# Sample attention: one gather per sequence for the cached pages, its first data fetched during the prompt's attention

## The reference

```python
def page_step(carry, pg):
    phys = page_table[:, pg]
    cos, sin = rope_tables(pg * PAGE_SIZE + jnp.arange(PAGE_SIZE))
    k, v = mla_keys(pool_ckv[layer, phys], pool_kpe[layer, phys], cos, sin, w_ukv, g_kn)
    s = jnp.einsum('bqhd,bkhd->bhqk', q, k) * SCALE
    return update(carry, s, v), None
```

## Time and profile before

| what | value |
|---|---|
| median of 3 runs | 4077.51 us (4075.68 to 4077.66) |
| the profiled execution's own time | 4077.87 us |
| its span in the trace | 4076.2 us |
| TensorE busy, share of the span | 3731.2 us, 92% |
| prompt attention | 1679 to 2212.9 us of the span |
| sample attention, setup | 2212.9 to 2261.6 us |
| sample attention, sequences and tail | 2261.6 to 2755.2 us |

### The profile page before, as it was taken

One profiled execution on the slowest core, in us unless ns is written; L12 is line 12 of the kernel. 1 busy time (PEld: TensorE's weight loads), 2 busy tenths in 40 slices (PEclk: granted clock), 3 DMA queues, 4 the chain that ended last, 5 costly groups with the idle time before them and its releaser, 6 DMA issues. The chain is left out here.

```text
span 4076.2 us, 76494 instructions
## 1 busy us (share of the span) xinstructions
PE 3731.2 (92%) x30291; PEld 2436.7 (60%) x30291; DVE 2036.8 (50%) x3709; ACT 1347.8 (33%) x2324; POOL 545.1 (13%) x809
## 2 busy tenths in 40 slices
PE   7879999999999999699997798886999998799899
PEld 4546666666666666466665455554777777455444
DVE  5773234444333333366564466654666665233353
ACT  4431013232232332255453455543545544000000
POOL 1000000000000000011112555512111121000000
PEclk9989999999999999899998899987999999899999
DMA  4422112222222221311212111104111111523342
GB/s 151 109 67 59 63 64 79 75 77 79 73 79 75 77 79 57 90 43 43 53 31 53 42 47 41 45 23 144 37 43 43 43 27 23 179 101 119 117 143 91
DMA packets 313767, 293.64 MB, mean 72 GB/s; under 512 B 90647, under 2 KB 274605, under 8 KB 300109
## 3 DMA queue, kind: packets, MB, share of 16 engines
q1 hardware_dynamic: 296572, 263.16, 20.9%
q0 software_dynamic: 14544, 25.46, 2.2%
q10 hardware_dynamic: 2304, 0.26, 0.0%
HBM read 181.38 MB, written 107.42 MB: 71 GB/s over the span
## 5 line engine op out<-in xcount | busy, mean ns | idle before, releaser
L325 PE MATMUL z_acc<-z_hx,ahead_ws 128*128 128x352 f32 x1872 | 558.0, 459 | 0.0
L543 DVE TENSOR_TENSOR z_st<-z_st,z_acc 128x1056 f32<-128x1056 f32 x208 | 254.0, 1253 | 589.0 <-PE z_acc L325 589.0
L325 PEld LDWEIGHTS z_acc<-z_hx,ahead_ws 128*128 128x128 f32 x1872 | 355.7, 190 | 198.1
L325 PE MATMUL z_acc<-hT,ahead_ws 128*128 128x352 f32 x1248 | 376.9, 459 | 0.0
L325 PE MATMUL z_acc<-hT,ahead_wt 128*128 128x352 f32 x1248 | 373.4, 459 | 0.0
L1166 PE MATMUL a_S<-a_kh,a_qb 96*128 96x512 f32 (+3 forms) x640 | 283.8, 538 | 38.2 <-DMA a_kh<-kT 29.4
L325 PEld LDWEIGHTS z_acc<-hT,ahead_ws 128*128 128x128 f32 x1248 | 236.8, 190 | 135.5 <-issue 7.7
L325 PEld LDWEIGHTS z_acc<-hT,ahead_wt 128*128 128x128 f32 x1248 | 237.1, 190 | 132.1
L1493 PE MATMUL s_kn<-s_wuk,s_ckT 128*128 128x512 f32 x528 | 293.4, 638 | 6.4 <-ACT s_sq L1571 5.0
L415 ACT ACTIVATE z_st<-z_acc 128x1056 f32<-128x1056 f32 x104 | 103.7, 1050 | 448.9 <-PE z_acc L325 448.9
L2689 PE MATMUL m_acc<-branches_o,m_wb 128*128 128x424 f32 (+1 forms) x640 | 231.2, 523 | 21.2 <-DMA m_wb<-in_w_ob 21.2
(11 more groups left out here) (401 smaller groups left out, 6470.8 us busy)
## 6 DMA issues: line engine op xcount, KB each, us to landing
ahead_wt<-in_w_in SPq DMA_DIRECT2D x52, 512.0 KB, 5.1
gT<-z_st SPq DMA_DIRECT2D x24, 1056.0 KB, 5.7
m_sg<-gT SPq DMA_DIRECT2D x24, 1056.0 KB, 9.4
zT<-z_xm SPq DMA_DIRECT2D x17, 1056.0 KB, 4.0
s_ck<-in_cache_ckv SPq DMA_DIRECT2D x256, 64.0 KB, 1.8
zT<-z_st SPq DMA_DIRECT2D x12, 1056.0 KB, 6.6
r_xs<-zT SPq DMA_DIRECT2D x48, 256.0 KB, 3.3
mT<-m_macc SPq DMA_DIRECT2D x8, 1056.0 KB, 5.3
```

Source lines behind the costliest of these rows:

```text
L325: last = nc.tensor.matmul(acc[slot][:, i, 0:CH3], w[:, k], HB[m][:, k, i * CH3:(i + 1) * CH3], start=(k == 0), stop=(k == KH - 1))
L543: tt(y, y, src, ALU.add if sign > 0 else ALU.subtract).then_inc(took_v, 1)
```

## The change

1. **One gather a sequence.** An index tile `sd_rows` is made once on POOL: four copies of the page table, times 4, plus the number of the quarter. One indirect transfer per sequence then fetches all latents (partition `32 r + n` gets quarter `r` of page `n`, 32 tokens, 16 KB in a row) and one all rotary keys (4 KB a partition). The tokens so lie in another order in the tile, and the rotary table `cos_old`/`sin_old` is permuted to match. POOL issues both; SP keeps only the two small transfers of the new tokens.
2. **Data set up earlier.** The loads of the setup, the index, and the gathers of sequences 0 and 1 stand in the prompt's attention: SP issues its part after `store(4)`, POOL its part ahead of row 6, and the key arithmetic of sequence 0 ahead of row 12.
3. **Three buffers of latents** in place of two, without the column of ones. The sum of the weights, which that column gave, is now a `tensor_reduce` of DVE (`lsum`) and a product with one column on PE.
4. **No loop.** All 8 sequences are written out.

```diff
@@ prompt attention, SP
                     store(m)
+                    if m == 4:
+                        data.load(sp, A, zT, qT)
+                        sp.wait_ge(data.blank, 1)
+                        for b in range(2):
+                            data.load_new(sp, O, b, False)
+                            data.load_new(sp, O, b, True)
@@ prompt attention, POOL
                 for m in range(NROW):
+                    if m == 6:
+                        data.index(g)
+                        for b in range(2):
+                            data.gather_keys(g, A, b)
+                            data.gather_latents(g, A, b)
+                    if m == 12:
+                        g.wait_ge(data.w_in, 16 * 13)
+                        data.keys(g, 0)
                     g.wait_ge(rl_ready, m + 1)
@@ new class SampleData
+    def index(self, g):
+        for u in range(2):
+            g.memset(self.ck[u][:, NPG], 0.0)
+        g.memset(self.kp[:, :, NPG], 0.0)
+        g.memset(self.kr[:], 0.0).then_inc(self.blank, 1)
+        g.wait_ge(self.idx_in, 16 * 5)
...
+    def gather_latents(self, g, A, b):
+        g.indirect_dma_start(self.ck[b % 3][:, 0:NPG].rearrange("p t c -> p (t c)"), None, A["cache_ckv"][0].rearrange("n (r t) c -> (n r) (t c)", r=4),
+                             bass.IndirectOffsetOnAxis(ap=self.rows[:, b:b + 1], axis=0)).then_inc(self.ck_in[b % 3], 16)
...
@@ sample attention, POOL
-                steps(g, step)
+                for b in range(DB):
+                    if b:
+                        if b >= 2:
+                            g.wait_ge(ss_total, (b - 1) * NG)
+                        data.keys(g, b)
+                    if b + 2 < DB:
+                        data.gather_keys(g, A, b + 2)
+                    if 2 <= b + 1 < DB:
+                        if b + 1 >= 3:
+                            g.wait_ge(pv_done, b - 1)
+                        data.gather_latents(g, A, b + 1)
@@ sample attention, PE
-                        pe.wait_ge(kr_ready, b + 1)
...
+                        pe.wait_ge(data.kr_r, b + 1)
+                        pe.wait_ge(data.ck_in[b % 3], 16 * (b // 3 + 1))
+                        pe.wait_ge(data.ckn_in[b % 3], 16 * (b // 3 + 1))
@@ sample attention, PE, soft, g == 5
-                        nc.tensor.matmul(mi[0:HQ, 0:KVR + 1], fold[:], pvs[:], start=True, stop=True).then_inc(fold_done, 1)
+                        nc.tensor.matmul(mi[0:HQ, 0:KVR], fold[:], pvs[:], start=True, stop=True)
+                        pe.wait_ge(lsum_ready, b + 1)
+                        apart(pe, idle_pe)
+                        nc.tensor.matmul(mi[0:HQ, KVR:KVR + 1], lsum[:], ones[:, 0:1], start=True, stop=True).then_inc(fold_done, 1)
@@ sample attention, DVE, soft, g == 4
+                        nc.vector.tensor_reduce(lsum[:], sc[:, u].rearrange("p n q -> p q n"), AX.X, ALU.add).then_inc(lsum_ready, 1)
```

More of the change, by code:

```diff
@@ L1300, in sample_attention_phase @@
+def sample_attention_phase(nc, A, O, ident, ocT, data):
+    with Phase(nc, "s") as p:
+        wuv, wuk, gk, qs, qpe, fold, cg = data.wuv, data.wuk, data.gk, data.qs, data.qpe, data.fold, data.cg
+        data.ck.append(p.sb("ck2", [P, NK, KVR]))
+        ck, kr, ss_pe, w_in = data.ck, data.kr, data.ss_pe, data.w_in
+        lsum = p.sb("lsum", [P, HQ])
         qabs = p.sb("qabs", [P, DB, HQ])
         qpe4 = p.sb("qpe4", [P, 4, DB, HQ])
-        cosk = p.sb("cosk", [P, NK, ROPE])
-        sink = p.sb("sink", [P, NK, ROPE])
@@ L1338, in sample_attention_phase @@
         mi = p.ps("mi", [P, W])
[L1339 to L1346, removed]
+        const_set, setup_pe, setup_done, lsum_ready = (p.sem(n) for n in ("cst", "spe", "sdn", "lsm"))
+        t_done, ct_copied, kn_done, squared, summed, sc_done, sc_out = (
+            p.sem(n) for n in ("td", "ctc", "knd", "sqd", "smd", "scd", "sco"))
+        idle_pe = p.sem("idpe")
+        soft_chain, ss_total, rt_ready, mx_ready, mxT_done, diag_ready, mb_done = (
+            p.sem(n) for n in ("sfc", "sst", "rtr", "mxr", "mxt", "dgr", "mbd"))
         sub_ready, exp_ready, pv_done, an_ready, anT_done, anT_copied, pair_done, o_copied = (
@@ L1351, in sample_attention_phase @@
         th_ready, fin_ready, stored = p.sem("thr"), p.sem("fnr"), p.sem("str")
-        tok = slice(T, T + NS)
-        ckv_pool, kpe_pool = A["cache_ckv"][0], A["cache_kpe"][0]
         pages = [list(range(4 * g, min(4 * g + 4, NK))) for g in range(NG)]
         def steps(eng, step):
[L1358 to L1363, removed]
-        def has_pages(s):
[L1366 to L1378, removed]
+            for s in range(DB + 1):
+                step(s, s % 2, s // 2)
+        def has_pages(s):
+            return s < DB
         def has_soft(s):
-            return not (isinstance(s, int) and s == 0)
+            return s > 0
         with nc.Block() as block:
@@ L1385, in _ @@
             def _(sp):
[L1386 to L1397, removed]
-                sp.wait_ge(const_set, 2)
[L1400 to L1408, removed]
+                sp.wait_ge(const_set, 2)
+                for b in range(2, DB):
+                    sp.wait_ge(ss_total, (b - 1) * NG)
+                    data.load_new(sp, O, b, False)
+                    if b >= 3:
+                        sp.wait_ge(pv_done, b - 2)
+                    data.load_new(sp, O, b, True)
                 sp.wait_ge(fin_ready, 1)
-                sp.dma_start(ocT[:, :, tok].rearrange("n p t -> p n t"), oS[:]).then_inc(stored, 16)
+                sp.dma_start(ocT[:, :, T:T + NS].rearrange("n p t -> p n t"), oS[:]).then_inc(stored, 16)
                 sp.wait_ge(stored, 16)
@@ L1427, in _ @@
                 g.affine_select(out=new_mask[:], in_=new_mask[:], compare_op=ALU.is_ge, fill=NEG, base=0,
                                 pattern=[[0, H], [1, TS]], channel_multiplier=-1).then_inc(const_set, 1)
[L1429 to L1457, removed]
@@ L1511, in soft @@
                             half = slice(page % 2 * HQ, page % 2 * HQ + HQ)
-                            last = nc.tensor.matmul(mi[half, 0:KVR + 1], sc[:, u, page], ck[:, u, page], start=(page < 2), stop=(page >= NK - 2))
+                            last = nc.tensor.matmul(mi[half, 0:KVR], sc[:, u, page], ck[b % 3][:, page], start=(page < 2), stop=(page >= NK - 2))
                         last.then_inc(pv_done, 1)
@@ L1542, in _ @@
             def _(act):
-                act.wait_ge(pt_in, 16)
-                act.wait_ge(const_set, 2)
-                load(act, 0, kp[:, 0], kpe_pool, O["s_kpe"], lambda page: kp0_in, range(NK // 2))
                 act.wait_ge(w_in, 16 * 13)
                 nc.scalar.activation(th[:], cg[:], ACT.Tanh, scale=0.5).then_inc(th_ready, 1)
-                act.wait_ge(const_set, 3)
+                act.wait_ge(const_set, 2)
                 def copies(b, u, g):
@@ L1566, in squares @@
                     r = (u + g) % 2
-                    if not isinstance(b, int) or b * NG + g >= 2:
+                    if b * NG + g >= 2:
                         act.wait_ge(summed, b * NG + g - 1)
@@ L1605, in _ @@
                     if q == 0:
-                        v.wait_ge(const_set, 3)
+                        v.wait_ge(const_set, 2)
                         v.wait_ge(w_in, 16 * 13)
@@ L1632, in scores @@
                     v.wait_ge(sc_done, b * NG + g + 1)
-                    if g == 0 and not (isinstance(b, int) and b < 2):
+                    if g == 0 and b >= 2:
                         v.wait_ge(pv_done, b - 1)
+                        v.wait_ge(lsum_ready, b - 1)
                     nc.vector.tensor_tensor(own.rearrange("p n (h t) -> p n h t", h=H), scp[r][:, 0:k].rearrange("p n (h t) -> p n h t", h=H),
@@ L2914, in build @@
             trunk_phase(nc, A, O, hT, ident, zT, gT, oaT, later, ahead)
-        prompt_attention_phase(nc, A, ident, zT, qT, kT, v_d, ocT, later.outs)
-        sample_attention_phase(nc, A, O, ident, zT, qT, ocT)
+        with ExitStack() as middle:
+            data = SampleData(nc, middle)
+            prompt_attention_phase(nc, A, O, ident, zT, qT, kT, v_d, ocT, later.outs, data)
+            sample_attention_phase(nc, A, O, ident, ocT, data)
         with ExitStack() as back:
@@ L2940, in consts @@
     new = np.concatenate([row + P * np.arange(NB)[None, :], PAST + row % TS], 1)
-    old = np.concatenate([row + PAGE * np.arange(NPG)[None, :], PAST + row % TS], 1)
+    old = np.concatenate([row % NPG * PAGE + row // NPG * NPG + np.arange(NPG)[None, :], PAST + row % TS], 1)
     cn, sn = rope_rows(new)
@@ L2951, in consts @@
     col = np.arange(W)[None, :] + 0 * t
-    return dict(cos_new=cn, sin_new=sn, cos_old=co, sin_old=so, rw_masks=masks, rw_levels=levels,
+    return dict(cos_new=cn, sin_new=sn, cos_old=co, sin_old=so, page_quarter=(row // NPG).astype(np.float32), rw_masks=masks, rw_levels=levels,
                 rw_bones=(t // HD == np.arange(P)[None, :] // HD).astype(np.float32),
```

120 lines of the change are left out of this document (85 added, 35 removed).

## The result

The changed kernel takes 4050.33 us at the median (4046.41, 4047.13, 4053.53 and 4053.54), 0.9935 of the time before, 95% interval 0.9918 to 0.9953: faster by 0.65%. Forecast were 4013 us, at most 4038. The sign came out, the size did not: the profiled executions differ by 31.5 us (4077.87 to 4046.41) where the sum said 64.2. The profiled execution of the changed kernel is the fastest of its four; by the medians the difference is 4 to 5 us smaller.

The account below looks back on a forecast made before the run. POOL's list of fetches and arithmetic was taken to bound the sample attention, with TensorE behind it. Terms of -81.8 us there and +17.6 in the prompt's attention took 4077.87 to 4013.7, forecast 4013 us, range 3998 to 4038.

Parts of the forecast that it names:

- POOL's waits and the half-clock starts: Sample attention: TensorE's wait for POOL's keys goes, gain 34.4 us, and starts at half clock go, gain 10.5.
- X = 18: Price in us of one gather on POOL at which the whole gain is gone; rival of a dear gather, chance 0.05.
- Moved contention I price at 0: Sample attention: POOL's arithmetic slowing DVE at a sequence's start instead of its end costs 0, as DVE has idle time.
- What remains is the chain 2225.20 to 2234.64: Setup of the sample attention: only TensorE's 9.4 us up to the folded queries remain, gain 39.3 us.
- I take 8, nearer to that: Prompt's attention, row 9: TensorE stalls 8 us for `a_qb`, queued behind the loads and beside the gathers.
- the worst case: Prompt's attention, row 9: `a_qb` lands at 1769.5 after all loads and gathers, a stall of 18 us.
- POOL in the prompt's attention: Gathers ahead of row 6 fall inside the `a_qb` stall; arithmetic of sequence 0 stalls TensorE 5.6 us at row 12.
- the clock was priced at 4: Prompt's attention: TensorE's clock falls after each of two stalls, 2 us lost each.
- The sum of weights: Sample attention: `lsum` is hidden on DVE; the extra one-column product and its wait cost TensorE 0.3 us, 8 times, 2.4.
- the gathers hold the prompt's attention: Rival: `a_qb` or row 6's sums come 18 to 26 us late, 4023 to 4031 us; chance 0.17.
- TensorE waits for DVE: Rival: between sequences DVE's sum, root and copy stay late, +18 to +27, 4031 to 4040 us; chance 0.13.

Follow-up runs that it names:

- e6: The changed kernel with loads, gathers and early arithmetic spread over the prompt's rows, and without POOL's arithmetic in sequences 2 to 7: 3995.51 us (one run).
- e2: Against the changed kernel, POOL's arithmetic for a sequence starts once four groups of the sequence before are summed: 4026.68 us, ratio to before 0.9878.
- e3: Against the changed kernel, loads, gathers and the arithmetic of sequences 0 and 1 are spread over the prompt's rows: 4013.36 us, ratio to before 0.9847.

## Why the prediction was wrong, step by step

- **POOL's waits and the half-clock starts: right.** No wait of TensorE for POOL between sequences is left, the clock at the boundaries is 1.00, and the first two turns with group 0 take 7.3 us (7.5 forecast). Over sequences 1 to 6 the clock is 0.98, since it now falls behind group 2 in three of them. A gather holds POOL 0.95 to 1.08 us, far below X = 18.
- **"Moved contention I price at 0": wrong, the largest miss in the sample attention.** DVE's idle third did not help, because what was locked out stood at the head of a chain: maximum, sum, root, copies, TensorE. From the first start to the last the terms allowed 374.1 us (416.9 less 34.4, 10.5 and, for the sums of seven sequences, plus 2.1); the change took 388.6, e6, without the arithmetic, 366.3. So the contention cost 22.3 us where the forecast had 0, and 7.8 of it was made good because without it sequence 0 needs 49.4 us and those from 2 on 52.7, not 53.4. Of the 14.5 us that are left, the tail behind the last start won back 2.1. The rule cited there, that of the Trainium skill, "SBUF — State Buffer", "Who interferes with whom", calls the shared ports an exclusive lock; the ends of L1675 and L1681, within 0.1 us of POOL's, agree. I had read it as a stretch that moves, and not looked at what stands behind the locked operation at its new place.
- **"What remains is the chain 2225.20 to 2234.64": wrong by 8.7.** Beside TensorE's transposes ran not only POOL's clears, as the step said, but the whole arithmetic of sequence 1, which the change puts right behind them. e2 and e3 took it away, and the setup was 10.1 and 10.3. That copies of DVE can need the shared ports too, the Trainium skill says as well, "SBUF — State Buffer", "Who interferes with whom"; the trace agrees (9.9 us for 1.7). The prediction had weighed operations with two SBUF inputs alone.
- **"I take 8, nearer to that": wrong, and the worst case was right.** The step that failed is the 8 us for `a_qb` of row 9: the wait was 16.9. The value was taken by likeness to a row with 2.6 MB in flight in SP's own queue, where here the gathers ran in a second queue beside it. From 1754 to 1763 SP's queue had 5.3% of the time of the DMA engines, and `a_qb` landed 1.4 us behind the last gather. That the worst case, 1769.5, fits the 1768.98 measured is in part luck: it let all 7.3 MB move from 1739.49 at 244 GB/s, while the gathers went out from 1745.82 and then moved at 420. Without the gathers the wait was 4.8 (3.5 forecast). The rule set against the change, "DMA: Bandwidth & Descriptors", "Queues, rings and completion order" of the Trainium skill, says that a DMA engine goes round its queues packet by packet; the trace agrees, with 352 packets of each queue and 3.65 MB against 0.12.
- **POOL in the prompt's attention: right.** 5.7 at row 12 (5.6), and its gathers were out ahead of row 6's sums. TensorE was busy 7.0 longer, at a lower clock, where the clock was priced at 4.
- **The sum of weights: nothing instead of 2.4** as long as DVE is not locked out: the two groups around the fold, from one transpose of the keys to the next, last 5.82 and 5.34 us before the change, 5.88 and 5.33 after it. Its length, 3.8 us, is what makes it a burden behind a late maximum.

Together: 10.7 more in the prompt's attention, 8.7 in the setup, 12.4 in the sequences and the tail, 0.9 outside; 64.2 less 32.7 is the 31.5 measured. By cases, the rival "the gathers hold the prompt's attention" came true in its place. The rival "TensorE waits for DVE" had the right chain at the wrong place: it is late in group 2, behind the moved arithmetic, and not between two sequences. The contention in the setup no case had, and none had two of them together.

## What to carry to other kernels

When guests move into a stage whose bound engine has no slack, ask which transfers of other queues are in flight when the host's next load goes out, and how large their rows are: here the load came through only behind the last gather. Spread the guests a row at a time: the same bytes and the same arithmetic cost 28 us in two lumps and nothing in pieces. When POOL's work on SBUF moves, list what DVE does at the new place with two SBUF inputs, or as a copy from SBUF to SBUF, allow for the length of a POOL instruction at each, and follow the chain behind it; idle time of DVE is no cover for that.

## What the hardware showed unexpectedly

- An operation of DVE on 128x64 numbers takes 0.23 us, or, begun beside a POOL instruction of 2.4 us, as long as that one still runs: 2.1 and 2.5. The four copies of 32x512, one SBUF input each, are held up too (9.9 us for 1.7); reductions (2.28 and 3.8 us) and the scaling of the scores, with one operand in PSUM (0.42), are not.
- Two DMA queues took turns packet by packet, whatever the packets' size: 352 each in 9 us, 3.65 MB of gathers against 0.12 MB of small loads.
- An indirect gather of 128 rows costs POOL about the same for the keys (0.98 us) as for the latents (0.95), which are four times the bytes.
- A wait of 2.7 us was followed by a clock of 0.50 in some sequences and not in others, 1.7 us each time; what decides it no run told apart.
